# Mixer 1: transposes of the second head in a bank of the scores, values ahead of scores, the distance bias spread by six transfers

## The reference

```python
def token_mixing(h, w_in, rel_bias, ..., w_out, lambda_init):
    proj = h @ w_in                       # 1024 -> 3072
    ...
    o_a = chunk_band_attention(...)       # 6 heads, softmax(q k / 8 + bias[rel]) v
    o_b = diff_attention(...)             # 4 heads, two softmax maps each, subtracted
    o_c = stick_breaking_attention(...)   # 6 heads, sigmoids and a running product
    y = jnp.concatenate([o_a, o_b, o_c], axis=-1)
    return y @ w_out
```

## Time and profile before

| | |
|---|---|
| median of 3 runs | 3346.61 us (3342.95 to 3347.3) |
| the profiled execution | 3347.98 us |
| its span, from the first to the last instruction | 3346.0 us |
| TensorE busy | 3286.6 us (98%) |
| VectorE, ScalarE, GpSimd busy | 1999.8, 1504.6, 294.5 us |
| mixer 1, scores to last values | about 407 to 625 us in layer 0, 1407 to 1628 us in layer 1 |

### The profile page before, as it was taken

The page is one execution under the profiler, slowest core; times in us unless marked ns, Lnnn a source line. Parts: engine busy times, 40 slices in busy tenths (PEclk is TensorE's granted clock), DMA queues, the critical chain, the costliest instruction groups (busy, mean ns, idle before and its releaser), DMA issues.

```text
span 3346.0 us, 56193 instructions
## 1 busy us (share of the span) xinstructions
PE 3286.6 (98%) x22486; PEld 2940.1 (88%) x22486; DVE 1999.8 (60%) x2730; ACT 1504.6 (45%) x2560; POOL 294.5 (9%) x161
## 2 busy tenths in 40 slices
PE   8999999999999999999999999999999999999998
PEld 7887876789889888876788889889999998899998
DVE  6664556676727664556676726746665277476643
ACT  5333445553425333445553434465443255754432
POOL 1000022100010000022100011210000022100000
PEclk9999999999999999999999999999999999999999
DMA  4343311233332332311233332212222321123222
GB/s 120 100 128 98 108 57 57 70 89 100 91 103 89 100 100 91 105 57 57 70 88 100 93 103 76 58 54 76 94 88 91 105 65 53 58 82 94 88 89 89
DMA packets 330744, 287.56 MB, mean 86 GB/s; under 512 B 9698, under 2 KB 326202, under 8 KB 330582
## 3 DMA queue, kind: packets, MB, share of 16 engines
q1 hardware_dynamic: 330117, 284.17, 28.3%
q10 hardware_dynamic: 464, 1.10, 0.1%
HBM read 283.10 MB, written 5.27 MB: 86 GB/s over the span
## 4 chain that ended last, share of the span: by engine, by line
PE 92%; DVE 4%; ACT 3%; issue 1%; DMA 1%; ACTq 0%; SPq 0%; DVEq 0%
PE ps L657 19%; PE ps L658 18%; PE ps L659 18%; PE ps L710 7%; PE ps L708 7%; PE ps L709 7%; PE ps L763 2%; PE ps L2167 2%; PE ps L2169 2%; PE ps L2168 2%; PE ps L1752 1%; PE ps L767 1%; PE ps L1791 1%; PE ps L1776 1%; PE ps L2217 1%
## 5 line engine op out<-in xcount | busy, mean ns | idle before, releaser
L645 DVE TENSOR_TENSOR wlo<-raw,whi 128x1024 fp32r<-128x1024 f32 x340 | 407.1, 1197 | 790.0 <-ACT whi L638 786.4
L657 PE MATMUL ps<-xhi,whi 128*128 128x512 f32 (+2 forms) x2512 | 839.1, 334 | 0.0
L658 PE MATMUL ps<-xlo,whi 128*128 128x512 f32 (+2 forms) x2512 | 828.2, 330 | 0.0
L659 PE MATMUL ps<-xhi,wlo 128*128 128x512 f32 (+2 forms) x2512 | 825.8, 329 | 0.0
L638 ACT ACTIVATE whi<-raw 128x1024 fp32r<-128x1024 f32 (+1 forms) x421 | 434.6, 1035 | 657.5 <-PE ps L659 561.9
L657 PEld LDWEIGHTS ps<-xhi,whi 128*128 128x128 f32 x2512 | 474.2, 189 | 58.2 <-issue 17.2
L659 PEld LDWEIGHTS ps<-xhi,wlo 128*128 128x128 f32 x2512 | 472.8, 188 | 45.1
L658 PEld LDWEIGHTS ps<-xlo,whi 128*128 128x128 f32 x2512 | 473.9, 189 | 39.4 <-issue 0.5
L657 PE MATMUL ps<-hhi,whi 128*128 128x512 f32 (+2 forms) x1056 | 359.7, 341 | 7.3 <-issue 7.3
L658 PE MATMUL ps<-hlo,whi 128*128 128x512 f32 (+2 forms) x1056 | 358.7, 340 | 0.0
L659 PE MATMUL ps<-hhi,wlo 128*128 128x512 f32 (+2 forms) x1056 | 358.4, 339 | 0.0
(11 more groups left out here) (327 smaller groups left out, 7002.1 us busy)
## 6 DMA issues: line engine op xcount, KB each, us to landing
raw<-in_ffn_w_up_dram SPq DMA_DIRECT2D x176, 512.0 KB, 3.7
raw<-in_ffn_w_down_dram SPq DMA_DIRECT2D x120, 512.0 KB, 3.5
raw<-in_w_in_dram SPq DMA_DIRECT2D x94, 512.0 KB, 3.8
raw<-in_ffn_w_gate_dram SPq DMA_DIRECT2D x88, 512.0 KB, 3.8
raw<-in_w_out_dram SPq DMA_DIRECT2D x32, 512.0 KB, 3.5
raw<-in_ffn_w_down_dram SPq DMA_DIRECT2D x24, 256.0 KB, 2.7
tbias_scratch<-rev_scratch SPq DMA_DIRECT2D x1, 3072.0 KB
y<-tbias_scratch SPq DMA_DIRECT2D x6, 512.0 KB, 4.7
```

What stands on the lines that cost most here:

```text
L645: eng.tensor_tensor(lo[:, 0:n], raw[slot][:, 0:n], hi[:, 0:n].bitcast(F32), ALU.subtract).then_inc(b.s.weights_split, 1)
L657: pe.matmul(o, wh, hi[:, t0:t0 + w], start=first, stop=False)
L658: pe.matmul(o, wh, lo[:, t0:t0 + w], start=False, stop=False)
L659: ins = pe.matmul(o, wl, hi[:, t0:t0 + w], start=False, stop=last)
```

## The change

One DMA becomes six of 512 KB, each behind one of the six loads of the second pair (`m == 1`) of the first down projection; the wait for them in mixer 1 counts all six. In mixer 1 the transposes of the second head go to bank 4 or 6 (`tbank`), a bank that held the scores of unit `u + 1`, where that unit and the next are not of kind B (`apart`: units 0 to 9 and 19 to 31). There they stand right behind those of the first head on TensorE, wait for the release of those scores (`scores_free`) in place of the copy of the first head, and the scores three units later wait for their copy. For units 10 to 18 they stay where they were. ScalarE's copy of the second head moves ahead of its splits and sigmoids in the same units. The values (`pv`) move ahead of the scores in every step.

```diff
--- before.py
+++ after.py
@@ -987,13 +987,14 @@
                     load_raw(sp, b, f.gb(l) + 4 * i + q, q % 2, up_rows(i, q), (4, PAIR))
             if first:
                 sp.wait_ge(s_revd, 16)
-                b0 = rev_dram[0:1, P - 1:P]
-                src = bass.AP(tensor=b0.tensor, offset=b0.offset, ap=[[640, 12], [-1, P], [1, SEQ]])
-                sp.dma_start(tbias_dram, src).then_inc(s_tbias, 16)
             for m in range(DOWN_PAIRS):
                 for q, k in enumerate(DOWN_Q):
                     src = f.down[bass.ds(l * FF + q * 512, k * P), m * PAIR:(m + 1) * PAIR]
                     load_raw(sp, b, f.gb(l) + UP_GRAN + 6 * m + q, q % 2, src, (k, PAIR))
+                    if first and m == 1:
+                        b0 = rev_dram[2 * q:2 * q + 1, P - 1:P]
+                        src = bass.AP(tensor=b0.tensor, offset=b0.offset, ap=[[640, 2], [-1, P], [1, SEQ]])
+                        sp.dma_start(tbias_dram[2 * q:2 * q + 2, :, :], src).then_inc(s_tbias, 16)
 
         def pe_up_granule(pe, b, l, f, i, q, between=None):
             g = f.gb(l) + 4 * i + q
@@ -1675,7 +1676,7 @@
                 if p == 1:
 
                     sp.wait_ge(e.norm_sums, pre(3 * l + 1, 1))
-                    sp.wait_ge(s_tbias, 16)
+                    sp.wait_ge(s_tbias, 6 * 16)
                     for h in (0, 2, 4):
                         sp.dma_start(tb[:, h:h + 2, :],
                                      tbias_dram[l * 6 + h:l * 6 + h + 2, :, :].rearrange("h p c -> p h c")).then_inc(
@@ -1699,6 +1700,15 @@
         def unit1(u):
             p, j = divmod(u, 4)
             return p, j, KINDS[p], P * (j + 1)
+
+        def apart(u):
+
+
+            return all(KINDS[v // 4] != "B" for v in (u + 1, u + 2) if v < UNITS1)
+
+        def tbank(u, h):
+
+            return 4 + 2 * ((u + 1) % 2) if h == 1 and apart(u) else 2
 
         def pe_mix1(pe, l):
             b, s = b1, b1.s
@@ -1744,6 +1754,8 @@
                 p, j, kind, n = unit1(u)
                 pe.wait_ge(s.columns_out, l * 24 + 3 * p + 2 + CR)
                 pe.wait_ge(s.scores_free, U + u + (2 if "B" in KINDS[p] + KINDS[max(u - 1, 0) // 4] else 1))
+                if u >= 3 and apart(u - 3):
+                    pe.wait_ge(s.transposed_out, TE + TEV1["p", u - 3, 1] + 2)
                 maps = 2 if kind == "B" else 1
                 rows = 64 // maps
                 for h in range(2):
@@ -1771,9 +1783,13 @@
                 p, j, kind, n = unit1(u)
                 if h == 0:
                     pe.wait_ge(s.probs_done, U + u + 1)
-                pe.wait_ge(s.transposed_out, TE + TEV1["p", u, h] + 1)
+                if h == 1 and apart(u):
+                    pe.wait_ge(s.scores_free, U + min(u + 2, UNITS1) + CR)
+                else:
+                    pe.wait_ge(s.transposed_out, TE + TEV1["p", u, h] + 1)
                 for t in range(j + 1):
-                    ins = pe.transpose(ps[:, 2, P * t:P * t + P], m1.w[u % 3][:, h, P * t:P * t + P], ident[:, :])
+                    ins = pe.transpose(ps[:, tbank(u, h), P * t:P * t + P], m1.w[u % 3][:, h, P * t:P * t + P],
+                                       ident[:, :])
                 ins.then_inc(s.transposed, 1)
 
             def pv(u):
@@ -1806,6 +1822,10 @@
             for st in STEPS1:
                 for u in st.tr:
                     ptrans(u, 0)
+                    if apart(u):
+                        ptrans(u, 1)
+                for u in st.pv:
+                    pv(u)
                 if st.sc == 0:
                     fill(st.tiles[:4])
                     pe_pre_sum(pe, sub, 1)
@@ -1814,10 +1834,9 @@
                     scores(st.sc)
                 if st.sc != 0:
                     fill(st.parts[0])
-                for u in st.pv:
-                    pv(u)
                 for u in st.tr:
-                    ptrans(u, 1)
+                    if not apart(u):
+                        ptrans(u, 1)
                 if st.sc != 0:
                     fill(st.parts[1])
                 if st.extra is not None:
@@ -1862,8 +1881,8 @@
                 act.wait_ge(s.transposed, TE + TEV1["p", v, h] + 1)
                 if v >= 2:
                     act.wait_ge(s.pv_done, U + v - 1)
-                act.activation(m1.pt[v % 2][:, h, :, :].rearrange("p a b -> p (a b)")[:, 0:nn], ps[:, 2, 0:nn],
-                               ACT.Copy).then_inc(s.transposed_out, 1)
+                act.activation(m1.pt[v % 2][:, h, :, :].rearrange("p a b -> p (a b)")[:, 0:nn],
+                               ps[:, tbank(v, h), 0:nn], ACT.Copy).then_inc(s.transposed_out, 1)
 
             def exps(u):
                 p, j, kind, n = unit1(u)
@@ -1903,13 +1922,16 @@
             for n_step, st in enumerate(STEPS1):
                 for v in st.tr:
                     transposed(v, 0)
+                    if apart(v):
+                        transposed(v, 1)
                 for g in st.done_in[0]:
                     if g < 24:
                         hi_split(g + 2)
                 if st.sc is not None and KINDS[st.sc // 4] == "C":
                     sigmoids(st.sc)
                 for v in st.tr:
-                    transposed(v, 1)
+                    if not apart(v):
+                        transposed(v, 1)
                 if st.sc is not None and KINDS[st.sc // 4] != "C":
                     exps(st.sc)
                 for p_ in st.pairs:
```

## The result

| | before | after |
|---|---|---|
| median | 3345.2 us of 4 runs | 3380.8 us of 4 runs (3376.14 to 3382.21) |
| span of the profiled execution | 3346.0 us | 3379.3 us |
| first big matmul of the first down projection to the first scores of mixer 1 | 149.7 us | 183.0 us |
| first scores to last values of mixer 1, layer 0 | 216.5 us | 216.2 us |
| the same, layer 1 | 220.0 us | 216.5 us |

The changed kernel takes 1.0104 times as long (95%: 1.0087 to 1.0122), 35.6 us more. 3340 was forecast with an upper end of 3346.5; that is wrong in sign and far out of the range.

What follows compares the result with a forecast made beforehand. TensorE, 92% of the chain, was taken as the bound. Bias 4.1 + mixer 1 2 x 2.1 + clock 1.5 - 2 x 1.2 = 7.4 us gained, forecast 3340 us, 8-in-10 range 3332 to 3346.5.

Steps and rivals of the forecast that it cites:

- part 1: Bias transfer, layer 0's first feed-forward: splitting it removes the late load at the down projection; 4.1 us gained, once.
- the cover of 3.4 us: Down projection's second pair: ScalarE waited 3.4 us per weight buffer for TensorE, so loads behind small transfers were taken as hidden.
- spreading only moves the collision: Rival, chance 0.12: six loads late by 0.7 us each take back the 4.1 us; 3344.5 us.
- The last sentence of the prediction: Prediction is wrong if pv 28 doesn't wait, regular steps are no shorter, or ScalarE waits for loads near 290 us.
- The gain at the handover: TensorE's start of layer 0's first down projection: gap 3.92 to 1.49 us, plus 1.6 to 1.7 for the clock; 4.1 us.
- Part 2: Regular step of mixer 1: 5.45 to 5.29 us by one shape change less, two unseen handovers assumed; 2.2 us a layer.
- Part 3: Mixer 1: value transposes' waits for the second head's copy go; with regular steps, 3.7 us a layer ahead before the tail.
- Part 4: Tail of mixer 1: values 28 wait about 4 us for VectorE's deferred copy, holding scores 31; 2.1 us a layer left.
- Part 5: Clock in mixer 1's tail: +1.5 us in layer 1, but new waits bring the lower clock, -1.2 us a layer.
- The +1.5 for layer 1: Clock gain in layer 1's tail of mixer 1, as the two 1 us waits around the value transposes get shorter.
- the tail isn't held: Rival, chance 0.16: pair 6's copy isn't late when pv 28 arrives; 4.9 us a layer, 3333 us.
- The rival of the void change: Rival, chance 0.08: transposes wait for the scores' bank, or unseen handovers eat the step gain (62 steps x 0.12); 3348 us.

Runs made afterwards that it cites:

- run 3: Changed kernel, but each of the six bias transfers takes 21 or 22 positions of all 12 rows instead of 2 rows; 3341.8 us, ratio 0.9992.
- run 4: Changed kernel, but each of the six bias transfers takes 64 positions of 4 rows, still 512 KB; 3345.8 us, ratio 1.0006.
- run 8: Kernel before with only the bias changed, to six transfers of 12 rows (21 or 22 positions each), mixer 1 as before; 3343.6 us, ratio 0.9993.
- run 9: As run 6, but the bias is one transfer of 12 rows at its old place ahead of the down projection's loads; 3334.3 us.
- run 12: The program of run 6 measured once more, as comparison; 3333.2 us, ratio 0.9963 to the kernel before.
- run 6: As run 3, but in step 31 alone the values stand again behind the scores and two tiles; 3330.9 us, ratio 0.9958.
- run 7: As run 3, but the values stand behind the scores and two tiles in every step, second head's bank kept; 3335.3 us, ratio 0.9968.
- run 1: Kernel before with only the bias changed, to six transfers of 2 rows (512 KB each), mixer 1 as before; 3378.1 us, ratio 1.0105.
- run 5: As run 3, but VectorE's output copy of pair 6 is not deferred (DEFER1 = (27,)); 3336.2 us, ratio 0.9975.
- run 11: As run 6, but the output copy of pair 6 is not deferred either; 3336.2 us, ratio 0.9975.

## Why the prediction was wrong, by its own steps

**The step that failed is in part 1: "I take 0; if the cover is gone, each of six costs up to 1 us, 6 us in all."** Its working took a transfer of 512 KB to run like a load of 512 KB, 2 to 3 us, and set that against the cover of 3.4 us. The transfer took 10.2 to 10.5 us, because its outer dimension was 2 and so two of the 16 engines carried it. The price is the stretch from the first big matmul to the first scores: 183.0 us after, 148.2 in run 3, 34.8 us in all or 5.8 each. 24.3 of them are waits of TensorE, and the other 10.5 I put down to the lower clock: 0.87 over 107 us is 13.9 us, some of which fell into the waits. The cover was not the step that failed: run 4's transfers of 5.1 us each (512 KB at 102 GB/s) cost 5.0 us in all on the same stretch (153.2 for 148.2), 0.8 each, so some 4.3 us of each were covered. The rival "spreading only moves the collision" had the right mechanism with a price of 0.7 a load from the same assumption. The "each up to 1 us" was no bound but the same guess again: the only transfer of the bias in the trace before had 12 rows and ran at 297 GB/s, and nothing there showed one with 2. The last sentence of the prediction, that ScalarE waiting for the loads near 290 us would show it wrong, named the place.

**The gain at the handover (4.1 us)** is in the profile as worked out: the gap 1.50 us for 3.92, then full clock (149.69 us to the first scores before, 148.2 in runs with full clock). But it was sized from one execution in which TensorE came early. The medians of runs 8, 9 and 12 give 1.1 to 1.4 us, with intervals that hold both.

**Part 2, the regular step.** In the profile after (TensorE, layer 0), eight transposes take 0.97 us, the values 0.81, the scores 0.63, and twelve big matmuls 2.88: the 5.29 us forecast, so the two unseen handovers together cost what was assumed. **Part 3:** the waits for m_pt are gone. Ahead of the transposes of unit 23 the kernel after had gained 2.1 us (2.6 forecast), ahead of those of unit 27 3.25 us (3.7 forecast). New waits for the copy of v (4.4 us in 5 times, before 2.2 in 2) took the difference. Runs 6 and 7 bear out what these parts give to each edit: with the values behind the scores nothing is gained up to step 25, and the gain of the bank comes at the transposes of v. What they left out is that the bank also shortens the tail, by 1.5 us behind step 30 in run 7, where nothing holds it.

**Part 4, the new wait,** is right to the place and the size: values 28 wait 3.96 us for VectorE's deferred copy ("about 4 us"), scores 31 behind them. **Part 5, the clock:** 0.83 over the tail in both layers, so the lower clock was a cost, as forecast. Together parts 4 and 5 were to give back 1.6 + 1.2 = 2.8 us a layer; from the first transposes of step 29 to the last values layer 0 took 26.5 us instead of 23.5, 3.0 more. Sum of a layer: 0.9 forecast, 0.3 measured. The +1.5 for layer 1 was an accident of one execution: in run 1 the old order had full clock there (216.7 us). The two waits of about 1 us (0.78 us of idle time each) to which part 5 ascribed the slow stretch stood in all six layers of the old order, and two of the six had it.

The rival "the tail isn't held" was priced at 4.9 us a layer; run 6, in which it isn't, brought 5.1 (216.5 to 211.4). Its own times give that too: 619.97 - 617.5 is 2.5, not 2.3. The rival of the void change counts 62 steps, where part 2 has 36 regular ones in the two layers; neither slip touches the forecast.

Had the six transfers cost nothing, the kernel would have been that of run 3: 3341.8 us. That looks like 2 us from the forecast of 3340, but it is in part luck. Of the 7.4 us forecast, run 3 has 3.3 (2.7 by its ratio, whose interval holds zero); the kernel before came out 1.5 us below the 3346.6 from which the forecast started. The handover and the +1.5 of layer 1 were sized from one execution.

## What to carry to other kernels

Before a DMA is cut into pieces, look at the outermost dimension of the pieces: cut so that it stays large (here along the positions, with all 12 rows in each piece), and check the rate of a piece in the DMA view before counting it as hidden. A transfer that is slow costs through the loads queued behind it, and a reserve of a few microseconds per load covers it only up to that length. A gain read from one profiled execution can be that execution's accident: look for the same place in a second profile. When a step is moved ahead of another, look for the one place in the loop where its wait is longest and leave the old order there: one exception in step 31 was worth 4.8 us a layer.

## What the runs showed of the hardware that I had not expected

- A DRAM to DRAM transfer in runs of 2 KB went at 25 GB/s for each unit of its outer dimension: 50, 102 and 297 GB/s at 2, 4 and 12, with 0.13, 0.26 and 0.79 of the 16 DMA engines busy. The loads behind it, on the same queue, were held up by its whole length through the shares of two engines, an eighth of each load; most of the load looked at had crossed in one burst some 5 us or more before.
- The clock at the start is not the same in every execution: 1.00 in the kernel before and 0.66 in the one after between 20 and 30 us, after the same wait of 2.8 us. It moves the arrival at 254 us by 2 to 3 us, and with it what a late load costs there (2.39 or 0.9 us of waiting).
- Waits of 3.96 us in the tail were followed by the lower clock in all eight layers that had them (0.83 over the last 20 us, 0.91 in layer 0 of run 3). Run 6, with waits of 1.3 and 0.9 us, had none in either layer; gaps of 1.05 and 1.58 us in run 5 were followed by it in layer 0 (0.91) and not in layer 1 (1.00), one of 2.29 us in run 11 in both (0.91).
